# V as 64-column weights in two column groups, joined one unit later, in three attention stages of a four-layer transformer

## The reference

```python
def joint_dense_attention(q, k, v, kc, vc):        # layer 1: mla (96-wide q, k) and gqa (64-wide)
...
    kk = jnp.concatenate([kc, k], axis=1)
    vv = jnp.concatenate([vc, v], axis=1)
...
        sc = jnp.einsum('bqkgd,bnkd->bkgqn', qi, kk, preferred_element_type=jnp.float32) * (d ** -0.5)
        p = jax.nn.softmax(sc, axis=-1)
        return jnp.einsum('bkgqn,bnkd->bqkgd', p.astype(vv.dtype), vv)
...
def joint_window_attention(q, k, v, kc, vc, sink): # layer 2: win, 64-wide, a window of 128 either side
...
        p = jax.nn.softmax(jnp.concatenate([s_ctx, s_loc, s_snk], axis=-1), axis=-1)
        return (jnp.einsum('bkgql,blkd->bqkgd', p[..., :l].astype(vc.dtype), vc)
                + jnp.einsum('bkgqm,bmkd->bqkgd', p[..., l:l + 3 * Q_BLOCK].astype(vi.dtype), vi))
```

## Time and profile before

| | us |
|---|---|
| device time, median of 3 runs | 1720.5 (1719.4 to 1723.0) |
| the profiled execution's own time | 1723.44 |
| its span (first to last instruction) | 1721.6 |
| mean granted clock of TensorE | 0.971 |
| PE busy | 1624.8 (94% of the span) |
| DVE busy | 899.1 (52%) |
| ACT busy | 647.5 (38%) |
| POOL busy | 566.9 (33%) |

### The profile page before, as it was taken

The page is one execution under the profiler, slowest core; times in us unless marked ns, Lnnn a source line. Parts: engine busy times, 40 slices in busy tenths (PEclk is TensorE's granted clock), DMA queues, the critical chain, the costliest instruction groups (busy, mean ns, idle before and its releaser), DMA issues.

```text
span 1721.6 us, 24787 instructions
## 1 busy us (share of the span) xinstructions
PE 1624.8 (94%) x9120; PEld 1342.5 (78%) x9120; DVE 899.1 (52%) x2120; ACT 647.5 (38%) x1320; POOL 566.9 (33%) x333
## 2 busy tenths in 40 slices
PE   4999889899999979999999999989999999999998
PEld 1788878797887858887888789956578778887787
DVE  2655737665554244924752688036531279916422
ACT  3322354354454323334542433344333343336322
POOL 1222231860001333446505344410424534431134
PEclk9999989899999989999999999969999999999999
DMA  8321212231013112331003232300112222220222
GB/s 326 83 73 46 62 50 87 71 90 50 26 38 111 62 31 80 93 97 57 1 1 101 86 98 83 90 0 1 50 49 86 95 86 98 98 74 1 80 92 86
DMA packets 93158, 124.40 MB, mean 72 GB/s; under 512 B 10288, under 2 KB 52208, under 8 KB 92016
## 3 DMA queue, kind: packets, MB, share of 16 engines
q1 hardware_dynamic: 93040, 122.82, 22.5%
HBM read 120.70 MB, written 2.10 MB: 71 GB/s over the span
## 4 chain that ended last, share of the span: by engine, by line
PE 86%; DVE 7%; ACT 3%; issue 2%; DMA 1%; POOL 1%; SPq 0%; DVEq 0%; ACTq 0%; POOLq 0%
PE psum L839 18%; PE psum L841 18%; PE psum L840 18%; PE psum L1032 10%; PE psum L997 8%; PE psum L1020 5%; PE psum L809 3%; PE psum L954 3%; DMA mod_w<-mod_w_in 1%; PE psum L994 1%; PE psum L898 1%; PE psum L999 1%; PE psum L995 1%; ACT rz L1188 1%; DVE row_rstd L1346 0%
## 5 line engine op out<-in xcount | busy, mean ns | idle before, releaser
L1757 POOL TENSOR_TENSOR wlo<-wraw,whi 128x1024 fp32r<-128x1024 f32 (+4 forms) x172 | 399.7, 2325 | 979.1 <-ACT whi L1083 979.0
L1083 ACT ACTIVATE whi<-wraw 128x1024 fp32r<-128x1024 f32 (+4 forms) x172 | 174.7, 1019 | 483.3 <-PE psum L841 483.3
L839 PE MATMUL psum<-whi,h2h 128*128 128x512 f32 (+2 forms) x800 | 309.3, 387 | 7.1 <-ACT buf L1132 5.9
L841 PE MATMUL psum<-whi,h2l 128*128 128x512 f32 (+2 forms) x800 | 305.8, 382 | 0.0
L840 PE MATMUL psum<-wlo,h2h 128*128 128x512 f32 (+2 forms) x800 | 305.5, 382 | 0.0
L839 PE MATMUL psum<-whi,hTh 128*128 128x512 f32 (+2 forms) x512 | 196.9, 385 | 9.5 <-DVE hTl L1454 7.3
L1226 ACT ACTIVATE pr<-psum,nmax 128x512 f32<-128x512 f32 (+1 forms) x208 | 137.9, 663 | 170.9 <-DVE nmax L1551 88.3
L841 PE MATMUL psum<-whi,hTl 128*128 128x512 f32 (+2 forms) x512 | 192.0, 375 | 0.0
L840 PE MATMUL psum<-wlo,hTh 128*128 128x512 f32 (+2 forms) x512 | 192.0, 375 | 0.0
L839 PEld LDWEIGHTS psum<-whi,h2h 128*128 128x128 f32 x800 | 150.7, 188 | 33.4 <-issue 8.0
L997 PE MATMUL psum<-kT,qT 64*128 64x256 f32 (+5 forms) x480 | 164.6, 452 | 7.1 <-DVE qT L1536 4.3
(11 more groups left out here) (253 smaller groups left out, 2459.8 us busy)
## 6 DMA issues: line engine op xcount, KB each, us to landing
wraw<-mod_w_in SPq DMA_DIRECT2D x32, 512.0 KB, 3.8
wraw<-w_in_odd_in SPq DMA_DIRECT2D x32, 512.0 KB, 3.4
wraw<-cd_w_in_in SPq DMA_DIRECT2D x24, 512.0 KB, 3.6
wraw<-w_in_even_in SPq DMA_DIRECT2D x20, 512.0 KB, 3.9
mod_w<-mod_w_in SPq DMA_DIRECT2D x8, 1024.0 KB, 17.8
wraw<-ab_w_in_in SPq DMA_DIRECT2D x16, 512.0 KB, 3.6
wraw<-w_ple_gate_in SPq DMA_DIRECT2D x16, 512.0 KB, 3.9
wraw<-ab_w_out_in SPq DMA_DIRECT2D x8, 512.0 KB, 3.6
```

The source lines that it names most:

```text
L839: eng.matmul(dst, a[0], ww[0], start=first, stop=False)
L841: mm = eng.matmul(dst, a[1], ww[0], start=False, stop=last_)
L1083: eng.activation(whi[:, s, :, 0:w], wraw[:, u["id"] % RAW, :, 0:w], ACT.Copy).then_inc(*to("split_hi", u["id"]))
L1757: eng.tensor_tensor(wlo[:, s, :, 0:w], wraw[:, u["id"] % RAW, :, 0:w], f32(whi[:, s, :, 0:w]), ALU.subtract)\
```

## The change

Three sets of names steer it. `HALVED` (gqa, mla, win): the product with V takes V, 64 columns, as weights, and 128 transposed exponentials of a block as moving columns. Blocks go by turns to rows 0 to 63 and 64 to 127 of bank 6, so that the bank holds two half sums of the transposed output; the second half's blocks come first. ACT copies these 128 by 128 values to `o2`, and one unit later a joining product with a new constant `halves` (two unit matrices of 64, one above the other) adds the halves and turns the result back; it lands in columns 256 to 319 of the second score bank of unit j−1, which no scores use. DVE's mix reads it from there, one unit later than before, and the loops are one iteration longer. `STACKED` now also has win: its scores are two fp32r products of 128 rows. `PARTED` (mla): high and low parts in four buffers, three fp32r products of 96 rows.

The order within an iteration changes for the three stages. On PE: scores(j), with the second bank waited for only at its first use; PV(j−2); the join of unit j−3; transposes of unit j−1, second half first; preparations; modulation. On ACT: the copy of o2 (j−2), second half (j−1), exponential (j), preparations. On DVE: low parts of a preparation that unit j needs, modc, nmax(j), mix(j−3), other low parts, first half (j−1). Preparations have a low part everywhere, and ACT makes the first high parts. Of the preparations within the loop, those at units 0 and 2 of each six go to bank 3 in gqa and mla; in gqa q's parts are spaced by two units. The modulation's steps of mla move from units 0 and 1 of each six to 4 and 5. The steps of `mla_norms` stand on odd units alone, the newton steps in lumps of three and two. In win the sink is an additional column of scores, written by a small fp32 product of the unit matrix with `nsink`, and `nsink` starts the row minimum, so that L1230, L1556 and L1576 are gone. Buffers are placed anew in SBUF to make room.

```diff
+    out["halves"] = np.concatenate([np.eye(64), np.eye(64)]).astype(np.float32)
...
+            n_, r = divmod(j, 2 if name == "gqa" else 6)
+            if name == "mla":
+                n_, r = n_ + len(units_of("gqa")) // 2, r - 4
+            return (("product", "turn")[r], ST["modb"][n_]) if 0 <= r < 2 and n_ < len(ST["modb"]) else None
...
-        STACKED = ("gqa",)
+        STACKED, PARTED = ("gqa", "win"), ("mla",)
+        ROUNDED = STACKED + PARTED
+        HALVED = ("gqa", "mla", "win")
...
-                nxt = when + 1
+                nxt = when + (2 if name == "gqa" else 1)
...
+            when = next(j for j in times if p_[0] in [q_[0] for q_ in times[j]])
+            return 3 if name in ("gqa", "mla") and when % 6 in (0, 2) else 7
+
+        def join_bank(i):
+            return score_bank(i) + 1
...
+                            elif name in PARTED:
+                                eng.matmul(dst, q_, ks[0:dk, a:b], start=True, stop=False)
+                                eng.matmul(dst, q_, kTl[0:dk, h % 2, a:b], start=False, stop=False)
+                                mm = eng.matmul(dst, qTl[0:dk, h % 2, t * P:(t + 1) * P], ks[0:dk, a:b], start=False, stop=True)
...
+                        if name == "win":
...
+                            c0 = s0 * 512 + cols_of(name, t)
+                            mm = eng.matmul(psum_flat[:, c0:c0 + 1], ident[:, :], nsink[:, h:h + 1], start=True, stop=True)
...
+                    if name in HALVED and lag < j <= n_units + lag:
+                        i = j - lag - 1
...
+                        bank_free(6)
+                        for p_, n_ in enumerate([*range(nb0, len(bl)), *range(nb0)]):
...
+                            c0 = 64 * (p_ % 2)
+                            mm = eng.matmul(psum[c0:c0 + 64, 6, 0:P], v_rows(name, h, bl[n_]), prT[:, i % 2, n_ * P:(n_ + 1) * P],
+                                            start=p_ < 2, stop=p_ >= len(bl) - 2)
+                        mm.then_inc(*to("product_v", (name, i)))
+                        reader[6] = ("o2_copied", (name, i))
+                    if name in HALVED and lag + 1 < j:
+                        i = j - lag - 2
+                        b = join_bank(j - 1)
+                        eng.wait_ge(*at("o2_copied", (name, i)))
+                        bank_free(b)
+                        eng.matmul(psum[:, b, 256:256 + dv], o2[:, i % 2, :], halves[:, :], start=True, stop=True)\
+                           .then_inc(*to("joined", (name, i)))
+                        reader[b] = ("mixed", (name, i))
...
+                    if name in HALVED:
+                        if lag < j:
+                            i = j - lag - 1
+                            eng.wait_ge(*at("product_v", (name, i)))
+                            eng.activation(o2[:, i % 2, :], psum[:, 6, 0:P], ACT.Copy).then_inc(*to("o2_copied", (name, i)))
+                        if lag <= j < len(units) + lag:
+                            second_half(j - lag)
+                        if j < len(units):
+                            exp(j)
+                        for p_ in preps.get(j, []):
+                            prep(p_)
...
+                    if name in HALVED:
+                        if lag + 1 < j:
+                            mix(j - lag - 2)
+                        for p_ in turned:
+                            if p_[1] > j:
+                                low(p_)
+                        if lag <= j < len(units) + lag:
+                            first_half(j - lag)
...
+                if j % 2 == 0 or j >= 32:
+                    return
+                n_, t = ("mq", "mk")[j // 16], j // 2 % 8
...
+                else:
+                    for r in ((0, 1, 2), (3, 4))[t - NT]:
+                        root_steps(n_, r)
```

More of the change, by code:

```diff
@@ L511, in temps @@
                 return qTs, kTs, pr1, prT1
-            return (qT1, kT1, pr1, prT1) if name in ("gqa", "mla", "win") else (qT2, kT2, pr2, prT2)
+            return (qTh, kTh, pr1, prT1) if name in PARTED else (qT2, kT2, pr2, prT2)
         def keys_of(name, g):
@@ L963, in attention @@
                 lag = LAG
-                for j in range(n_units + lag + 1):
+                for j in range(n_units + lag + 1 + int(name in HALVED)):
                     if j < n_units:
@@ new lines, in attention @@
+                    if name in HALVED and lag + 1 < j:
[6 more added lines that the diff above has]
+                        reader[b] = ("mixed", (name, i))
+                    for p_ in preps.get(j, []) if name not in HALVED else ():
@@ L1035, in attention @@
                         reader[6] = ("mixed", (name, i))
+                    for p_ in preps.get(j, []) if name in HALVED else ():
+                        prep(p_)
                     beside = modb_at(name, j)
@@ new lines, in mix @@
+                def mix(i):
+                    h, t = units[i]
+                    rs, ri = rsum[:, i % 4:i % 4 + 1], rinv[:, i % 4:i % 4 + 1]
+                    eng.wait_ge(*at("exps", (name, i)))
+                    eng.reciprocal(ri, rs).then_inc(*small())
+                    after_last()
+                    if name == "diff" and h % 2:
+                        eng.tensor_tensor(ri, ri, nlam[:, :], ALU.mult).then_inc(*small())
+                        after_last()
+                    eng.wait_ge(*at("joined" if name in HALVED else "product_v", (name, i)))
+                    o = psum[:, 6, 0:DV[name]]
+                    if name in HALVED:
+                        o = psum[:, join_bank(i + lag + 1), 256:256 + DV[name]]
+                    if name == "diff":
+                        dst = buf6[:, t, (h // 2) * P:(h // 2 + 1) * P]
+                        if h % 2 == 0:
+                            eng.tensor_scalar(dst, o, ri, None, ALU.mult).then_inc(*note("mixed", (name, i)))
+                        else:
+                            eng.scalar_tensor_tensor(out=dst, in0=o, scalar=ri, in1=dst, op0=ALU.mult, op1=ALU.add)\
+                               .then_inc(*note("mixed", (name, i)))
+                    else:
+                        c0 = {"gqa": 512 + h * 64, "mla": h * 64, "win": h * 64, "fox": 512 + h * P, "odd": h * P}[name]
+                        dst = rz[:, t, c0:c0 + DV[name]]
+                        eng.scalar_tensor_tensor(out=dst, in0=o, scalar=ri, in1=dst, op0=ALU.mult, op1=ALU.mult)\
+                           .then_inc(*note("mixed", (name, i)))
@@ L1538, in attention @@
+                for j in range(len(units) + lag + 1 + int(name in HALVED)):
+                    turned = preps.get(j - 1, []) if name in HALVED and j > 0 else []
+                    for p_ in turned:
+                        if p_[1] == j:
+                            low(p_)
                     step_ = modb_at(name, j - 1) if j > 0 else None
@@ new lines, in attention @@
+                    if name in HALVED:
+                        if lag + 1 < j:
+                            mix(j - lag - 2)
+                        for p_ in turned:
+                            if p_[1] > j:
+                                low(p_)
+                        if lag <= j < len(units) + lag:
+                            first_half(j - lag)
+                    else:
+                        if lag <= j < len(units) + lag:
+                            first_half(j - lag)
+                        if lag < j:
+                            mix(j - lag - 1)
```

191 lines of the change are left out of this document (87 added, 104 removed).

## The result

The changed kernel takes 1737.0 us (median, 1732.0 to 1739.4) where the kernel before takes 1721.9 (1719.4 to 1724.4): a ratio of 1.0081, 95% interval 1.0060 to 1.0103. It is 0.8% slower: 14 us by the ratio, 15 between these medians. 1709 was forecast, and 1722 was the upper end. The profiled execution's own time is 1733.6, its span 1731.8.

What follows compares the result with a forecast made beforehand. PE was taken to bound the kernel: 32.0 us less PE work, two thirds given back, left −0.5 (gqa), −8.2 (mla) and −2.7 (win), −11.4 in all. Forecast 1709.0 us, range 1692 to 1722.

Steps and rivals of the forecast that it cites:

- What bounds the kernel: Whole kernel: PE bounds it, with 86% of the chain of waits; DVE has 7%.
- Part 1, overlap of the groups: V product: two column groups overlap fully, so six blocks take 0.65 us instead of 1.3.
- Price of a unit: V product with join: 1.05 us for six-block units (−0.30), 0.62 for two-block units (+0.18).
- Part 2, scores: fp32r scores: −0.19 us per six-block mla unit, −6.1 in mla; win's scores 1.02 instead of 1.28 a unit.
- Part 3, gqa: gqa: work −6.1, modc waits −3.5, bank 3 +5.2, key group +1.9, newton roots +2: −0.5 us.
- The key group: Change of key group in gqa: about 6.4 us from scores' end to next scores, instead of 4.5: +1.9.
- the preparations' 4: mla: preparations in bank 3 make PE wait 0.5 us, 8 times: +4.
- win: win: work −13.1 us, returns +10.4 from start, key group, clock and sink: −2.7.
- B: Rival: the returns don't come, bank 3 being free and win's clock holding: 1695 us; chance 0.2.
- C: Rival: slower, the chain through ACT (exp, join, transposes, copies) sets the unit: 1735 us; chance 0.08.
- D: Rival: the two column groups don't run side by side, +65: 1774 us; chance 0.04.
- E: Rival: two to three more clock drops than counted, in gqa, mla or win: 1717 to 1722 us; chance 0.11.

Runs made afterwards that it cites:

- e_onegroup: The change with all V blocks in one column group, the o2 copy and join over 64 rows: 1809.0 us, run one time.
- e_ctx: The change with the 32 context units' V product as before, without o2 copy and join: 1729.9 us, ratio to before 1.0035.
- e_early: The change with preparations where they were before, right behind the scores on PE and all in bank 7: 1727.1 us, ratio to before 1.0031.
- e_scores_fix: e_scores with win's first high parts ahead of out2's weight slices and the second key preparation in bank 5: 1712.1 us, ratio to before 0.9936.
- e_best: e_scores_fix with newton steps one by one and q's preparations in adjacent units, as before: 1711.1 us, ratio to before 0.9935.
- e_last: e_early_all with out1's first weight slice rounded on ACT behind mla's last exponential: 1708.0 us, ratio to before 0.9918.
- e_scores: The change without its V part (`HALVED` empty), order and mix as before, preparations in bank 7: 1734.5 us, ratio to before 1.0041.
- e_stops: The change with win's first high parts ahead of out2's weight slices and the second key preparation in bank 5: 1728.5 us, ratio to before 1.0032.
- e_early_all: e_early plus e_ctx's context product, e_stops' shortened stops, single newton steps and q's preparations adjacent: 1712.9 us, ratio to before 0.9947.

## Why the prediction was wrong, step by step

**What bounds the kernel** was right: PE. e_onegroup and e_ctx show PE's work passing into time. What was wrong is how much PE would save, and what of its new idle time would be exposed.

**Part 1, overlap of the groups**: taken as full; right (e_onegroup). **Price of a unit**: the step that failed first. The forecast had 1.05 us for X and 0.62 for C; the rows say 0.90 + 0.27 = 1.17 and 0.46 + 0.27 = 0.73. The two changes of form at 0.09 were right. What the sum lacked is that the first fp32 record behind each change holds PE 0.16 instead of 0.11: once in the tiled product and once in the join, whose two records make 0.27 and not 0.22. That is 0.11 a unit, in 128 units 14 us, and it fits PE's busy time, which fell by 19 us where 32 was forecast. The V part alone, priced so, is 32 × 0.17 − 16 × 0.29, or about 1 us a stage in gqa and mla, where −6.1 and −6.7 were forecast. In mla it turned out as a small loss: 16.79 a head (e_early) against 16.49 (e_scores_fix), where −0.84 was forecast.

**Part 2, scores**: the direction was right and the size too small. From before to e_scores_fix a head of mla without a gate step loses 1.15 us, against 0.76 forecast (one with a gate step 0.62), and win goes from 102.8 to 94.5, though its start and key group cost more than before.

**Part 3, gqa**: the wait of bank 3 was priced at 5.2 and the roots at 2; together they are 14.4 [the first list of the result]. The step looked at DVE's row minimum alone, and not at a DVE queue made late by a slow step beside GpSimd, which PE now meets at the mix. The spacing of q's preparations, priced at nothing, costs too: spacing and lumps together are 4.0 us of gqa (e_best against e_scores_fix). The key group took 7.5 us from the start of the row minimum to the next scores, against 6.4.

**mla**: the preparations' 4 was about 1.3, but the modulation product, which was moved to units 4 and 5 and priced at 0, stands behind the low part of the preparation in bank 7 and waits 0.6 to 0.7 us in each head. The text spoke of SP's loads at that move and not of the bank; that is the term that was left out. The ledger of a head of mla without a gate step: 17.64, −1.15 (scores, e_scores_fix), +0.30 (V halves, e_early), +0.83 (late preparations, the modulation's wait among them, the change), makes 17.62. These are differences of runs, which add up by construction; what they show is the sizes. In a head with a gate step they are 18.53, −0.62, +0.35 and +0.29.

**mla's end**: not in the forecast. The last six units take 20.2 us, 17.7 before. ACT rounds out1's first slice behind the last o2 copy, PE waits 2.9, and runs at half clock behind it; e_last priced it at about 4 to 5 us.

**win**: start idle 6.5 us instead of 4.8 (a copy of k's low part, L1607, took 1.87 us beside GpSimd and 0.29 elsewhere in win), the key group 5.6 instead of 6.4; win lost 1.1 where −2.7 was forecast, mean clock 0.92.

The sum by terms: −11.4 forecast; +14 (price of a unit), +7 (gqa's waits), +3 (mla's modulation less the smaller wait of bank 3), +4 (mla's end), −4 (scores better than forecast), +3 to 4 (win) gives some +16. Two terms are missing there: mla's last six units, +2.5, and gqa's clock, which was at half for 13.7 us instead of 27.3, an estimated −7. With them it is some +12, where the two profiled executions, from which the terms are read, differ by 10 and the medians by 15. Each figure is from one profile, and clock drops move between executions by 4 us and more, so that the sum shouldn't be trusted to better than 5.

**The rivals.** B (the returns don't come) fell: they came, and larger. C (slower by the chain through ACT) is right in sign, and its 1735 beside 1737 is luck, for its mechanism is wrong: PE waits for prT and pr 0.6 us each in gqa. A DVE queue that comes late held PE, through banks 3 and 7. What the Trainium skill's page TensorEngine Tiling (Array Packing) says under PSUM Bottleneck, that tiling speeds up TensorE but not the evacuation of PSUM, fits only in the wide sense that the engines behind PE hold it. D fell with e_onegroup. E fell for the change, whose clock in gqa was better than before (0.96), and is true of e_scores. In the profile after, some of the signs named in the prediction showed it: PE L972 (the old L954) waiting for rz, the mla heads not shorter, and win's first scores 8.0 us after the stage's start, where 5 was named, with the clock at 0.74 in its first 20 us.

## What to carry to other kernels

A product in a tiled form pays for the way in, the way out, and the first record behind each; here that is 0.18 plus 0.10 a time, besides the join, and a unit with two blocks, which can save 0.22 at most, never earns it. When work is moved within hand-made queues, write down for each PSUM bank who reads it last and what stands ahead of that reader on its engine; some 10 us of the miss are in two such readers, beside the 14 of the products' price. And when PE is at full clock, price a stop of some us with the slow stretch behind it, as a range: shortening the stops gave 8 us (e_stops), while the V product at its best gave nothing clear of noise (e_early_all against e_best).

## What the runs showed of the hardware that was not expected

After a stop of about 3 us the clock stayed at its lower level (1.2 GHz) for some 38 us in e_scores, though PE had no gap, and another execution of the same program was 24 us shorter, with a mean clock of 0.964 instead of 0.951. At the same place, behind stops of 2.3 and 1.4 us in the change and 2.9 and 0.3 us in e_early, it was low for 6.8 us, and in e_scores_fix, behind 3.2 us, for 3.4. At mla's start stops of the same size left it low for 10.2 us in e_best and not at all in e_scores_fix. What decides stays open.

DVE operations on 48 columns took up to 1.85 us beside long GpSimd operations, against 0.38 to 0.50, and a copy of 512 columns (L1607) 1.35 us where it takes 0.48 in win.

Two column groups work at once: in the tiled product a record of each group starts every 0.11 us, as one record alone does in e_onegroup. And 64 moving columns in fp32 are no cheaper than 128: 0.215 us a block in the earlier trace rows, 0.22 a block in e_onegroup.
